# Splitting the reads of the sample states behind the first sequence's halves, sharing the page loads 12/11/9, and loading the first bias row a stage earlier, in a decoder step on one core

## The chip, the cores and the metric

The program runs on one NeuronCore of a Trainium2 chip. The metric is device time in microseconds (us), the median over several executions. Engines are called by their short names: PE (TensorE), ACT (ScalarE), DVE (VectorE), POOL (GpSimd) and SP (SyncE, which here only issues transfers). Everything is float32, and a float32 matmul stands in the trace as two matmul records with two weight loads.

## The reference, cut to what matters

One layer of a hybrid decoder is computed for a prompt of 1024 tokens and for 8 samples of 4 tokens. The change lies in the mLSTM of the samples and in the sparse attention:

```python
# mLSTM, one step for the samples (4 tokens each, 4 heads of 128)
num = sc[..., None] * einsum('bhvk,bhtk->bhtv', C, qc) + einsum('bhts,bhsv->bhtv', s, vc)
C = sc[..., -1, None, None] * C + einsum('bhs,bhsv,bhsk->bhvk', wl, vc, kc)

# sparse attention: each block of 32 cached tokens is compressed to one key and one value
blk = kb.reshape(B, nc, CMP_BLK, G, D) + pe[None, None, :, None, :]
flat = moveaxis(blk, 3, 2).reshape(B, nc, G, CMP_BLK * D)
kcmp = gelu(flat @ w1) @ w2      # and the same for the values
bias = rel_table[t5_bucket(dist)]  # added to every logit of the attention
```

For a sample the cached tokens lie in 32 pages of 128 tokens, scattered over a pool in DRAM. The page numbers are in `page_table`.

## The kernel before, in words

The whole step is one program of stages. Between two stages stands a barrier of all engines, ahead of which SP clears the semaphores of the stage one by one. Inside a stage each engine has its list of instructions written out by hand, and semaphores join the lists.

The change is in the joint stage `states_and_blocks` (tiles named `sab_...`), and in the stage behind it, `nsa_prompt` (tiles `np_...`). The joint stage does three things side by side:

- It compresses the cached blocks of 8 sequences. For sequence n the 32 pages (128 KB of each are needed) are loaded into `kv_in[n % 2]`, so there are two buffers. `load(eng, n, first, count, done)` issues one engine's share of the pages: for up to four pages at a time it reads the page numbers into registers (`value_load`, the TENSOR_LOAD rows), then issues one DMA per page. From n = 2 on the load waits until `layer1_ready` has reached 2(n-1), which is when PE has finished both halves of sequence n-2 and so released the buffer. PE then runs `first(n, 0)` and `first(n, 1)`, the first layer for keys and for values (64 matmul records each, helper `first_layer`), ACT applies the gelu, `second(n)` is the second layer, and DVE copies its result out (`blocks(n)`).
- It runs the mLSTM step of the samples: queries and keys, gates, `from_state` (the states C times the queries: 64 matmul records of 4 columns), `turn_inter`, `from_step`, `spread_scales`, and 8 `update(q)` of the states, which are put between the halves of the sequences.
- It does the prompt's own blocks (`own_first`, `own_second`, from the tile `sab_pairs`) and the vector of position biases: `bias_part` works in the tile `ring`, and SP writes the result to the DRAM scratch `bias_vec`.

The pages of a sequence are shared by the line

```python
SP_N, POOL_N, ACT_N = 14, 12, 6
```

The order of PE around the first sequences is written out:

```python
first(0, 0)
own_second()
from_state()
first(0, 1)
turn_inter()
first(1, 0)
```

ACT issues its pages behind the second gelu of the sequence whose buffer comes free, in the same list as its other work. `nsa_prompt` starts with SP loading two rows of `bias_vec` (one for each of two heads, 128 partitions x 1920 numbers each, read with a shift of one number from partition to partition) into `raw`. PE's first matmuls there wait for both rows, and nothing of the stage's attention starts before them.

Of the kernel before, what the change touches and what calls it, by code (L numbers as in the profile page):

```python
# [17 lines left out]
ACT = mybir.ActivationFunctionType  # L18
ALU = mybir.AluOpType
# [3 lines left out]
P = 128  # L23
# [904 lines left out]
RAWW = 1920  # L928
# [24 lines left out]
def states_and_blocks(nc, A, O, K, N, zn, hm, tokm, sm, pages, ring, tile_at, spare, c_at, psum):  # L953
# [6 lines left out]
    with stage(nc, "sab") as (ctx, sem):  # L960
# [7 lines left out]
        def dead(n, shape):  # L968
# [27 lines left out]
                 "updated", "norm_ready", "num_read", "square_ready", "root_ready", "gated_ready", "turned", "stored")  # L996
# [12 lines left out]
        SP_N, POOL_N, ACT_N = 14, 12, 6  # L1009
# [48 lines left out]
        def _(pe):  # L1058
# [150 lines left out]
        def _(act):  # L1209
# [10 lines left out]

            act.dma_start(mnorm[:, :, :], A["m_norm"].partition_broadcast(NS)).then_inc(S["small_loaded"], 16)
# [25 lines left out]
            gelu(0, 0)  # L1247
            act.wait_ge(S["inter_ready"], 1)
            nc.scalar.activation(inter[:, :, :], heads(psum[:, 7, 0:P]), ACT.Copy).then_inc(S["inter_copied"], 1)
            gelu(0, 1)  # L1250
            load(act, 2, SP_N, ACT_N, loaded)
            for n in range(1, NSEQ):
                gelu(n, 0)
                gelu(n, 1)
                if n == 1:
# [6 lines left out]
        def _(ve):  # L1262
# [62 lines left out]
            nc.vector.tensor_copy(N["vcmp"], psum[:, 2, P:2 * P]).then_inc(S["copied"], 1)  # L1325
            ve.wait_ge(S["inter_turned"], 1)
            ch.link(nc.vector.tensor_tensor(num[:, :, :], heads(psum[0:NS, 5, :]), per_head(sc[:, :], MD), ALU.mult))
            blocks(0)
# [15 lines left out]
            ve.wait_ge(S["inter_ready"], 1)  # L1344
            for n in range(1, 5):
                blocks(n)
                update(2 * n - 2)
                update(2 * n - 1)
# [2333 lines left out]
```

## Time and the profile before

| | us |
|---|---|
| median of 3 runs | 2687.54 |
| lowest, highest | 2683.41, 2691.82 |
| the profiled execution | 2690.47 |
| its span in the trace | 2688.8 |
| PE busy in the span | 2346.5 (87%) |
| joint stage, first DMA issue to last copy of DVE | 431.1 to 594.9 |
| start of the next stage, its first matmul | 598.7, 606.1 |

The profiled execution is one run, 2.93 us above the median. Times in the trace are counted from the start of the span. A row of the timeline merges neighbouring instructions of one line, so that its duration reaches from the start of the first to the end of the last. For a DMA on SP or ACT it is the time in which the engine issued them, not the time in which the data moved.

### The profile page before, as it was taken

To read this page: it belongs to the slowest core of one execution; us is meant where nothing else is said; L and a number is where in the kernel's file an instruction comes from. 1 tells how busy PE (TensorE), PEld (TensorE's weight loads), DVE (VectorE), ACT (ScalarE), POOL (GpSimd) and SP (SyncE) were. 2 spreads that over 40 slices of the span, in tenths; PEclk is the share of its full clock that TensorE was granted. 3 is DMA by queue.
4 is the path that set the end of the run, shared out by engine and by line. 5 is a ranking of instruction groups with operands and counts; after the bars stand their busy time and mean duration, and the time that the engine had idled before them with its cause. 6 is when DMAs were issued, how large, how long until landed. Compare 5 with 4: busy or idle time off the path is not lost. (4 is left out here: it accounts for less than half of the span.)

```text
span 2688.8 us, 41029 instructions
## 1 busy us (share of the span) xinstructions
PE 2346.5 (87%) x15785; PEld 2078.6 (77%) x15785; DVE 1086.2 (40%) x2456; ACT 691.7 (26%) x1391; POOL 393.8 (15%) x354
## 2 busy tenths in 40 slices
PE   8999676768999543999979988989999999999995
PEld 7799564665666321888879984879999999999995
DVE  2212453216777423211112610534755555553335
ACT  4210142004667211111113300344311111121123
POOL 0000021330000232111101110011122222212220
PEclk9999886788999766999989999999999999999997
DMA  3211205761300676111131013441211111111212
GB/s 130 106 40 40 14 1 172 229 232 60 122 22 1 206 245 220 37 35 47 39 112 32 32 48 109 195 154 53 76 55 48 48 48 42 45 38 48 106 42 73
DMA packets 118657, 228.71 MB, mean 85 GB/s; under 512 B 23666, under 2 KB 79635, under 8 KB 115299
## 3 DMA queue, kind: packets, MB, share of 16 engines
q1 hardware_dynamic: 85290, 171.55, 19.2%
q10 hardware_dynamic: 23970, 29.56, 3.2%
q0 software_dynamic: 9216, 25.18, 2.8%
q8 instruction: 114, 1.87, 0.3%
q14 instruction: 67, 0.55, 0.1%
HBM read 205.12 MB, written 25.31 MB: 86 GB/s over the span
## 5 line engine op out<-in xcount | busy, mean ns | idle before, releaser
L88 PE MATMUL psum<-x_half_high,ff_half 128*128 128x352 f32 x3240 | 790.9, 324 | 13.8 <-DVE h_again_low L69 8.9
L88 PEld LDWEIGHTS psum<-x_half_high,ff_half 128*128 128x128 f32 x3240 | 567.7, 189 | 15.1 <-DVE ff_half L69 9.1
L88 PE MATMUL psum<-h_again_low,ff_half 128*128 128x352 f32 x1176 | 379.2, 322 | 0.0
L69 POOL TENSOR_TENSOR ff_half<-ring,ff_half 128x1024 fp32r<-128x1024 f32 (+2 forms) x85 | 177.3, 2086 | 760.1 <-ACT ff_half L2987 760.1
L88 PEld LDWEIGHTS psum<-h_again_low,ff_half 128*128 128x128 f32 x1176 | 223.0, 190 | 0.0
L88 PE MATMUL psum<-x_half_high,mg_half 128*128 128x352 f32 x768 | 191.7, 330 | 22.2 <-ACTq L2117 22.2
L88 PE MATMUL psum<-merged_high,oq_half 128*128 128x352 f32 x768 | 190.8, 329 | 14.2 <-DVE oq_half L69 14.1
L2987 ACT ACTIVATE ff_half<-ring 128x1024 fp32r<-128x1024 f32 (+2 forms) x88 | 78.0, 888 | 433.1 <-PE psum L88 406.9
L88 PE MATMUL psum<-mid_low,ff_half 128*128 128x352 f32 x516 | 166.4, 323 | 0.0
L88 PEld LDWEIGHTS psum<-x_half_high,mg_half 128*128 128x128 f32 x768 | 135.1, 190 | 24.0 <-issue 22.4
L88 PEld LDWEIGHTS psum<-merged_high,oq_half 128*128 128x128 f32 x768 | 137.2, 193 | 15.1 <-DVE oq_half L69 14.7
L88 PE MATMUL psum<-h_high,in_half 128*128 128x352 f32 x528 | 126.1, 322 | 0.0
L88 PE MATMUL psum<-h_again_low,mg_half 128*128 128x352 f32 x384 | 124.1, 323 | 0.0
L2105 PE MATMUL psum<-low,mg_branch_w 128*128 128x352 f32 x384 | 116.2, 459 | 0.0
L88 PE MATMUL psum<-in_half,h_high 128*128 128x512 f32 (+3 forms) x360 | 102.1, 369 | 0.0
L938 PE MATMUL psum<-sab_kv,sab_w 128*64 128x128 f32 x1024 | 74.6, 316 | 31.0 <-DMA sab_kv<-in_pool 28.6
L2105 PEld LDWEIGHTS psum<-low,mg_branch_w 128*128 128x128 f32 x384 | 72.5, 190 | 37.2
L938 PEld LDWEIGHTS psum<-sab_kv,sab_w 128*64 128x64 f32 x1024 | 70.8, 164 | 35.7 <-DMA sab_kv<-in_pool 30.5
L3291 DVE TENSOR_TENSOR h_again<-h_again,psum 128x352 f32<-128x352 f32 x96 | 49.8, 520 | 119.4 <-PE psum L88 119.3
L88 PEld LDWEIGHTS psum<-mid_low,ff_half 128*128 128x128 f32 x516 | 97.6, 189 | 0.0
L1560 ACT ACTIVATE np_p<-np_p,np_nm 128x640 f32<-128x640 f32 (+7 forms) x128 | 92.7, 727 | 10.3 <-DVE np_nm L1632 10.0
L1511 PEld LDWEIGHTS psum<-consts,np_p 128*128 128x128 f32 x528 | 56.6, 142 | 49.9 <-DVE np_p L1662 21.1
(530 smaller groups left out, 3960.0 us busy)
## 6 DMA issues: line engine op xcount, KB each, us to landing
sab_kv<-in_pool SPq DMA_DIRECT2D x112, 128.0 KB, 3.5
sab_kv<-in_pool POOLq DMA_DIRECT2D x96, 128.0 KB, 3.8
ns_kv<-in_pool POOLq DMA_DIRECT2D x96, 128.0 KB, 4.6
ns_kv<-in_pool SPq DMA_DIRECT2D x96, 128.0 KB, 4.3
ring<-in_f_wu SPq DMA_DIRECT2D x22, 512.0 KB, 3.5
ring<-in_f_wg SPq DMA_DIRECT2D x22, 512.0 KB, 3.5
ns_kv<-in_pool ACTq DMA_DIRECT2D x64, 128.0 KB, 4.2
ring<-in_w_merge SPq DMA_DIRECT2D x16, 512.0 KB, 4.0
```

The source lines that it names most:

```text
L69: return engine.tensor_tensor(low, x, high.bitcast(F32), ALU.subtract)
L88: ins = nc.tensor.matmul(out, w[a], x[b], start=first and n == 0, stop=last and n == 2)
L938: last = nc.tensor.matmul(psum[g * HD:(g + 1) * HD, bank, 0:width], w1[:, kv, j, :], rows(g, j), start=(j == 0), stop=(j == CB // 2 - 1))
L1511: last = nc.tensor.transpose(psum[:, 4 + n % 2, c:c + P], src, K["ident"][:, :])
L1560: ins = nc.scalar.activation(x, x, ACT.Exp, bias=nm[:, b, g, i:i + 1], scale=-1.0, accum_out=sums[:, b, g:g + 1])
L2105: last = nc.tensor.matmul(acc[:, 3 + g, 0:GW], branch_w[:, r, k * P:(k + 1) * P], x[:, k, g * GW:(g + 1) * GW], start=(k == 0), stop=(k == 3))
L2987: nc.scalar.activation(half(u)[:, 0, 0:n], ring[:, u % 2, 0:n], ACT.Copy).then_inc(S["w_high"], 1)
L3291: ins = nc.vector.tensor_tensor(z[:, f, col(g)], z[:, f, col(g)], bank(v), ALU.add)
```

## The change

It has four parts. `from_state` takes a range of heads; heads 0 and 1 are read behind both halves of sequence 0, heads 2 and 3 behind `second(0)`. The items of the mLSTM step that follow it move on by one sequence (`update(0)` now stands in the pass of n = 3). The pages are shared 12 (SP), 11 (POOL), 9 (ACT). The two small transfers of `cmp_pe` into `sab_pairs` go from SP to the head of ACT's list. And the first of the eight bias rows is loaded in the joint stage, by SP behind its pages of sequence 2, into `ring`, which is free by then; in `nsa_prompt` the row for g = 0 always lives in `ring`.

```diff
-        SP_N, POOL_N, ACT_N = 14, 12, 6
+        SP_N, POOL_N, ACT_N = 12, 11, 9
...
             sp.dma_start(wqk[:, :, :, :], A["m_wqk"]).then_inc(S["wqk_loaded"], 16)
-            for g in range(2):
-                sp.dma_start(pairs[:, :, g, NPR:], A["cmp_pe"]).then_inc(S["pe_loaded"], 16)
...
             sp.dma_start(A["bias_vec"], onehot[0:NH, :]).then_inc(S["stored"], 16)
-            for n in range(2, NSEQ):
+            load(sp, 2, 0, SP_N, loaded)
+            sp.wait_ge(S["stored"], 16)
+            sp.dma_start(bias_row(ring, None)[0], bias_source(A, 0)).then_inc(S["raw_loaded"], 16)
+            for n in range(3, NSEQ):
                 load(sp, n, 0, SP_N, loaded)
+            sp.wait_ge(S["raw_loaded"], 16)
             sp.wait_ge(S["updated"], NSEQ)
...
-            def from_state():
+            def from_state(heads):
                 pe.wait_ge(S["C_loaded"], 16)
-                for h in range(MH):
+                for h in heads:
...
             first(0, 0)
             own_second()
-            from_state()
             first(0, 1)
-            turn_inter()
+            from_state((0, 1))
             first(1, 0)
             second(0)
+            from_state((2, 3))
+            first(1, 1)
+            turn_inter()
+            first(2, 0)
+            second(1)
             from_step()
-            first(1, 1)
+            first(2, 1)
             spread_scales()
-            for n in range(2, NSEQ):
+            for n in range(3, NSEQ):
                 first(n, 0)
                 second(n - 1)
-                if n < 6:
-                    update(2 * (n - 2))
-                if n == 6:
+                if n < 7:
+                    update(2 * (n - 3))
+                if n == 5:
                     turn_out()
                 first(n, 1)
-                if n < 6:
-                    update(2 * (n - 2) + 1)
+                if n < 7:
+                    update(2 * (n - 3) + 1)
...
+            for g in range(2):
+                act.dma_start(pairs[:, :, g, NPR:], A["cmp_pe"]).then_inc(S["pe_loaded"], 16)
             act.dma_start(mnorm[:, :, :], A["m_norm"].partition_broadcast(NS)).then_inc(S["small_loaded"], 16)
...
-            gelu(0, 0)
-            act.wait_ge(S["inter_ready"], 1)
-            nc.scalar.activation(inter[:, :, :], heads(psum[:, 7, 0:P]), ACT.Copy).then_inc(S["inter_copied"], 1)
-            gelu(0, 1)
-            load(act, 2, SP_N, ACT_N, loaded)
-            for n in range(1, NSEQ):
+            for n in range(NSEQ):
                 gelu(n, 0)
+                if n == 1:
+                    act.wait_ge(S["inter_ready"], 2)
+                    nc.scalar.activation(inter[:, :, :], heads(psum[:, 7, 0:P]), ACT.Copy).then_inc(S["inter_copied"], 1)
                 gelu(n, 1)
...
+def bias_row(ring, raw):
+
+    return ring[:, :, :].rearrange("p a k -> p (a k)")[:, 0:RAWW], raw
+
+
+def bias_source(A, h):
+    src = A["bias_vec"][h:h + 1, 0:RAWW]
+    return bass.AP(tensor=src.tensor, offset=src.offset, ap=[[1, P], [1, RAWW]])
...
-        raw = sb("raw", [P, 2, RAWW])
+        raw = bias_row(ring, sb("raw", [P, RAWW])[:, :])
...
-                    sp.dma_start(raw[:, g, :], src).then_inc(S["raw_loaded"], 16)
+                    if p or g:
+                        sp.dma_start(raw[g], bias_source(A, p + NPAIR * g)).then_inc(S["raw_loaded"], 16)
...
-                    pe.wait_ge(S["raw_loaded"], 32 * (p + 1))
+                    pe.wait_ge(S["raw_loaded"], 32 * p + 16)
```

On DVE the copies `blocks(0)` and `blocks(1)` and the updates move to match. The program's order of instructions shows it at three places. The first is PE, from the first half of sequence 0. Before (L938 is a half of a sequence, L1134 `from_state`, L1141 `turn_inter`, L1115 and L1116 `second`):

```order
L938 MATMUL psum<-sab_kv,sab_w_3303 64x128 x32
L1093 MATMUL psum<-sab_act_own,sab_w_3304 128x32
L1095 MATMUL psum<-sab_w_3304,sab_act_own 32x128 x4
L1134 MATMUL psum<-sab_qT,sab_C 128x4 x32
L938 MATMUL psum<-sab_kv,sab_w_3303 64x128 x32
L1141 MATMUL psum<-consts,sab_inter 32x128 x4
L938 MATMUL psum<-sab_kv,sab_w_3303 64x128 x32
L1115 MATMUL psum<-sab_act,sab_w_3304 128x128
```

The same place now (line numbers are those of the changed kernel, one higher or lower):

```order
L937 MATMUL psum<-sab_kv,sab_w_3303 64x128 x32
L1094 MATMUL psum<-sab_act_own,sab_w_3304 128x32
L1096 MATMUL psum<-sab_w_3304,sab_act_own 32x128 x4
L937 MATMUL psum<-sab_kv,sab_w_3303 64x128 x32
L1135 MATMUL psum<-sab_qT,sab_C 128x4 x16
L937 MATMUL psum<-sab_kv,sab_w_3303 64x128 x32
L1116 MATMUL psum<-sab_act,sab_w_3304 128x128
L1117 MATMUL psum<-sab_w_3304,sab_act 128x128
L1135 MATMUL psum<-sab_qT,sab_C 128x4 x16
L937 MATMUL psum<-sab_kv,sab_w_3303 64x128 x32
L1142 MATMUL psum<-consts,sab_inter 32x128 x4
```

The 32 matmuls of `from_state` have moved from ahead of the second half of sequence 0 to two places behind it, 16 each. The second place is the head of ACT's list in the joint stage. Before:

```order
L1208 UNCONDITIONAL_BRANCH
L1221 DMA sab_mnorm<-in_m_norm 32x512
L1222 DMA sab_n_3310<-in_s_n0t 32x512
L1223 DMA sab_n<-in_s_n 8x512
L1224 DMA sab_m<-in_s_m0t 32x4
L1018 TENSOR_LOAD pages
```

And now:

```order
L1213 UNCONDITIONAL_BRANCH
L1227 DMA sab_pairs<-in_cmp_pe 128x2x16 x2
L1228 DMA sab_mnorm<-in_m_norm 32x512
L1229 DMA sab_n_3310<-in_s_n0t 32x512
L1230 DMA sab_n<-in_s_n 8x512
L1231 DMA sab_m<-in_s_m0t 32x4
L1017 TENSOR_LOAD pages
```

Two transfers stand ahead of the four, and behind them ACT issues nine pages where it issued six, before its four copies into `sab_pairs` (`turn_pairs`). The third place is SP's list behind its last page of sequence 2, which is new:

```order
L1019 ISA
L1019 DMA sab_kv<-in_pool 128x256
L1042 DMA ring<-bias_vec 128x1920
L1017 TENSOR_LOAD pages
L1017 ISA x2
```

The bias row stands between the pages of sequence 2 and those of sequence 3.

## Rows read from the trace of the kernel before

**Rows 1.** The page: busy time and granted clock in 40 slices.

```profile
PE 2346.5 (87%) x15785; PEld 2078.6 (77%) x15785; DVE 1086.2 (40%) x2456; ACT 691.7 (26%) x1391; POOL 393.8 (15%) x354
PE   8999676768999543999979988989999999999995
```

**Rows 2.** Waits in the joint stage, 431 to 599; then SP's own waits.

```profile
PE psum L938 <- DMA sab_kv<-in_pool: 28.6, 6, 9.0
...
SPq L1018 <- PE psum L938: 16.1, 2, 13.0
...
SPq L123 <- DMA out_s_m<-sab_sl: 7.9, 1, 7.9
```

**Rows 3.** Timeline of PE, joint stage and after: start, duration, [idle before].

```profile
446.85 3.63 PE L938 MATMUL psum<-sab_pairs,sab_w 128*64 128x33 f32 x64
...
463.75 5.55 PE L938 MATMUL psum<-sab_kv,sab_w 128*64 128x128 f32 x64 [2.37 <-ACT sab_act_own L1244]
...
469.93 9.78 PE L1134 MATMUL psum<-sab_qT,sab_C 128*128 128x4 f32 x64
479.63 6.13 PE L938 MATMUL psum<-sab_kv,sab_w 128*64 128x128 f32 x64
...
491.52 3.71 PE L938 MATMUL psum<-sab_kv,sab_w 128*64 128x128 f32 x64
...
505.59 5.12 PE L938 MATMUL psum<-sab_kv,sab_w 128*64 128x128 f32 x64 [8.97 <-DMA sab_kv<-in_pool]
...
519.17 5.16 PE L938 MATMUL psum<-sab_kv,sab_w 128*64 128x128 f32 x64 [2.01 <-DMA sab_kv<-in_pool]
...
529.63 1.15 PE L1165 MATMUL psum<-tokm,sab_kwm 32*128 32x128 f32 x8
...
583.53 5.38 PE L938 MATMUL psum<-sab_kv,sab_w 128*64 128x128 f32 x64 [4.13 <-DMA sab_kv<-in_pool]
...
593.99 0.39 PE L1116 MATMUL psum<-sab_w,sab_act 128*128 128x128 f32 x2
606.08 6.08 PE L1485 MATMUL psum<-np_raw,consts 128*128 128x512 f32 x8 [11.71 <-DMA np_raw<-bias_vec]
```

**Rows 4.** Timeline of SP: issue of pages and transfers.

```profile
431.52 3.04 SPq L1033 DMA_DIRECT2D sab_pairs<-in_cmp_pe  x2
...
488.33 93.18 SPq L1020 DMA_DIRECT2D sab_kv<-in_pool  x84
581.56 0.43 SPq L1046 DMA_DIRECT2D out_s_C<-sab_C  x1
...
598.67 0.84 SPq L1434 DMA_DIRECT2D np_raw<-bias_vec  x2
```

**Rows 5.** Timelines of ACT and POOL: pages, copies.

```profile
437.07 4.35 ACTq L1020 DMA_DIRECT2D sab_kv<-in_pool  x6
441.47 2.65 ACT L1026 COPY sab_pairs<-zn 64x512 f32<-64x512 f32 x4 [16.27 <-issue]
...
488.10 4.07 ACTq L1020 DMA_DIRECT2D sab_kv<-in_pool  x6
...
493.46 2.29 POOL L1020 DMA_DIRECT2D sab_kv<-in_pool  x4 [2.24 <-issue]
```

**Rows 6.** DMA traffic in 490 to 503, then in 519 to 536.

```profile
DMA packets 3313, 4.01 MB, mean 308 GB/s; under 512 B 481, under 2 KB 2959, under 8 KB 3311
...
DMA packets 3917, 4.79 MB, mean 281 GB/s; under 512 B 569, under 2 KB 3480, under 8 KB 3916
```

**Rows 7.** Stretches: busy of PE, PEld, DVE (of sab_C's instructions), granted clock, DMA share, GB/s.

```profile
469.93:474.60 4.67, 4.67 (x41) 4.67 (x42) 0.00 (x0) 0.98 1.05 346
474.60:479.60 5.00, 5.00 (x24) 5.00 (x24) 0.00 (x0) 0.50 0.05 17
```

**Rows 8.** The bias rows' transfers: landing of the first, of the second (us).

```profile
np_raw<-bias_vec SPq DMA_DIRECT2D x1, 960.0 KB, 5.1
...
np_raw<-bias_vec SPq DMA_DIRECT2D x1, 960.0 KB, 7.0
```

More of the change, by code:

```diff
@@ L927 @@
 NCMP = TP // CB
-RAWW = 1920
 STRIPW, CSTRIPW, WSTRIPW = TP, NCMP + 4 * (NTILE - 1), WIN + P
@@ L995, in states_and_blocks @@
                  "inter_ready", "inter_copied", "inter_turned", "scale_ready", "scale_spread", "masked_ready", "update_ready",
-                 "updated", "norm_ready", "num_read", "square_ready", "root_ready", "gated_ready", "turned", "stored")
+                 "updated", "norm_ready", "num_read", "square_ready", "root_ready", "gated_ready", "turned", "stored", "raw_loaded")
         S = {n: sem(n) for n in names}
@@ L1325, in _ @@
             nc.vector.tensor_copy(N["vcmp"], psum[:, 2, P:2 * P]).then_inc(S["copied"], 1)
+            blocks(0)
             ve.wait_ge(S["inter_turned"], 1)
             ch.link(nc.vector.tensor_tensor(num[:, :, :], heads(psum[0:NS, 5, :]), per_head(sc[:, :], MD), ALU.mult))
-            blocks(0)
+            blocks(1)
             ve.wait_ge(S["intra_ready"], 1)
@@ L1343, in _, with nsa_prompt @@
             signal(nc.vector.tensor_tensor(n8[:, :, :], n8[:, :, :], heads(psum[0:NSEQ, 4, :]), ALU.add), "norm_ready")
-            ve.wait_ge(S["inter_ready"], 1)
-            for n in range(1, 5):
+            ve.wait_ge(S["inter_ready"], 2)
+            for n in range(2, 6):
                 blocks(n)
-                update(2 * n - 2)
-                update(2 * n - 1)
-            ve.wait_ge(S["root_ready"], 1)
-            ch.link(nc.vector.reciprocal(r1[:, :], r1[:, :]))
-            ch.link(nc.vector.tensor_tensor(num[:, :, :], num[:, :, :], per_head(r1[:, :], MD), ALU.mult))
-            ch.link(nc.vector.tensor_tensor(num[:, :, :], num[:, :, :], mnorm[:, :, :], ALU.mult))
-            signal(nc.vector.tensor_tensor(num[:, :, :], num[:, :, :], heads(tokm[0:NS, last, C_OG:C_OG + 512]), ALU.mult), "gated_ready")
-            blocks(5)
-            ve.wait_ge(S["turned"], 1)
-            nc.vector.tensor_copy(hm[:, :, TP:T], heads(psum[:, 5, 0:P]))
+                update(2 * n - 4)
+                if n == 2:
+                    ve.wait_ge(S["root_ready"], 1)
+                    ch.link(nc.vector.reciprocal(r1[:, :], r1[:, :]))
+                    ch.link(nc.vector.tensor_tensor(num[:, :, :], num[:, :, :], per_head(r1[:, :], MD), ALU.mult))
+                    ch.link(nc.vector.tensor_tensor(num[:, :, :], num[:, :, :], mnorm[:, :, :], ALU.mult))
+                    signal(nc.vector.tensor_tensor(num[:, :, :], num[:, :, :], heads(tokm[0:NS, last, C_OG:C_OG + 512]), ALU.mult), "gated_ready")
+                update(2 * n - 3)
+                if n == 4:
+                    ve.wait_ge(S["turned"], 1)
+                    nc.vector.tensor_copy(hm[:, :, TP:T], heads(psum[:, 5, 0:P]))
             blocks(6)
             blocks(7)
-def nsa_prompt(nc, A, O, K, N, zn, tokn, gates, on, psum):
+RAWW = 1920
+def bias_row(ring, raw):
[3 more added lines that the diff above has]
+    return bass.AP(tensor=src.tensor, offset=src.offset, ap=[[1, P], [1, RAWW]])
+def nsa_prompt(nc, A, O, K, N, zn, tokn, gates, on, ring, psum):
     BIAS = -1
@@ L1484, in scores @@
                                 c = slice(i * 512, i * 512 + w) if i < 2 else slice(CB - 1, CB + CB * (CSTRIPW - 1), CB)
-                                last = nc.tensor.matmul(out, K["flip"][:, :], raw[:, g, c], start=True, stop=True)
+                                last = nc.tensor.matmul(out, K["flip"][:, :], raw[g][:, c], start=True, stop=True)
                             elif br == CMP:
@@ L3479, in build @@
             assert place["blocks_kept"] == place["tokm"]
-            nsa_prompt(nc, A, O, K, N, zn, tokn, branch_gates, zm, psum)
+            nsa_prompt(nc, A, O, K, N, zn, tokn, branch_gates, zm, ring, psum)
             nsa_sample(nc, A, K, N, zn, tokn, branch_gates, pages, zm, psum)
```

5 lines of the change are left out of this document (1 added, 4 removed).

## The prediction

> **What bounds the kernel now.** I read the page first. PE is busy for 87% of the span, so most of the time is matmul work that this change doesn't touch; but its busy digits fall to 5, 4 and 3 in slices seven to ten, and its clock digits there to 6 and 7 [rows 1]. The joint stage lies in these slices, so I read only that stage. The list of waits says what PE lacks there: 28.6 us in six waits for pages of the cache, the longest 9.0 [rows 2]. The timeline of PE shows where they stand: ahead of the first half of each sequence from the third on, with 8.97 us at 505.59 and still 4.13 us at 583.53 [rows 3]. From 519.17 to 583.53 four sequences pass, 16.1 us each.
>
> Next, who is late with the pages. SP issues 84 of them in 93.18 us with hardly a pause, 1.11 us a page [rows 4], and in the whole stage it waits for PE only twice, 16.1 us together, 13.0 of them ahead of sequence 2 [rows 2]. So a load of 14 pages takes SP 15.5 us. POOL needs 2.29 + 2.25 = 4.5 us for four pages, 13.6 us for its twelve. ACT starts 2.3 us after the release at 485.76 (the end of the row at 479.63) and issues six pages in 4.07 us, 6.4 us in all, 1.07 a page, and is done long before the others [rows 3, 5]. SP is the last of the three by 2 us against POOL and by 9 against ACT. What remains, from the end of SP's issue to PE's start, I call the tail: 485.76 + 15.5 = 501.3, PE starts at 505.59, so 4.3 us.
>
> The other gate is the buffer. The pages of sequence 2 can only be issued once PE has finished sequence 0, at 485.76, and between its two halves stand the 9.78 us of reading the states [rows 3]. Meanwhile SP stands idle. The stretches show something more: in the first part of this read the granted clock was 0.98 of full speed, in the second 0.50, the lower of the two levels, 1.2 GHz [rows 7]. The first part did 41 matmul records in 4.67 us, the second 24 in 5.00, and the half sequence behind it took 6.13 us where a warm one takes 3.71 [rows 3, 7].
>
> **The change part by part.** Times on the old clock of the trace.
>
> *Opening.* ACT gets two small transfers at its head and three pages more. SP's own pair took 3.04 us, in which one issue had stalled [rows 4]; without a stall two cost about 0.6. Three pages cost 3 x 1.07 = 3.2. ACT's copies into the pairs ended at 441.47 + 2.65 = 444.1 [rows 5]; they will end at 447.9 to 450.3. PE needs them at 446.85 for the prompt's own blocks [rows 3], so a cover of 2.7 us is used up and PE comes 1.1 to 3.5 us later. I take +2.5, nearer the stall, since it has been seen with these very transfers. SP's list gets shorter, but nothing waits for its first pages: PE is late for other reasons. The release for sequence 1 moves with PE; its pages are still in time, because PE now comes to them later in its list.
>
> *Order.* Sequence 0: the first half starts at 463.75 + 2.5 = 466.3, ends 5.5 later, the prompt's second layer takes 0.7, the second half, now warm, 3.7: done at 476.2 against 485.76. Behind it stand half the state read (16 matmuls, 32 records: 3.6 us at full clock, 6.7 at half; I take 3.7, since warm halves now stand between them), a half of sequence 1 (3.7), the second layer (0.6), the other read (3.7) and the other half (3.7): sequence 1 is released at 491.6, and before it was at 491.52 + 3.71 = 495.2. Everything from the state read to the updates moves on by one sequence. DVE and ACT wait for it there, but both idle most of the stage, so I cost it at nothing.
>
> *Shares.* SP's load: 12 x 1.11 = 13.3 us, POOL's 12.5, ACT's 9 x 1.07 = 9.6. The time from release to PE's start was 19.8 for sequence 2. By the issue it becomes 13.3 + 4.3 = 17.6. By the data: 32 pages of 128 KB are 4.19 MB; in 490 to 503, when all three queues fed it, the traffic was 308 GB/s [rows 6], which makes 13.6 us; with 2.6 from the release to SP's first issue (488.33 [rows 4]) and 2.0, about half of the tail, for a page to be under way, 18.2. The later of the two counts: 18.2. Its bounds are 17.0 (the traffic rises as the shares get even) and 19.5 (281 GB/s, as in 519 to 536 [rows 6]).
>
> One rule of the Trainium skill speaks against this part: in "DMA: Bandwidth & Descriptors", section "Issuing engines are not separate DMA queues", it is said that issuing on several engines saves only the sequencers' time, usually small beside the transfer. Here 1.11 us on SP stands against 0.43 us of traffic for a page at 308 GB/s, so the trace doesn't agree with "small"; the rest of the rule is my first rival. By the same page's limit of about 358 GB/s for a core's HBM, an estimate for a sequence would be 11.7 us of traffic.
>
> *The sum in the stage.* PE needs 529.63 - 519.17 = 10.5 us from the start of a sequence to its release [rows 3]. With two buffers, sequences 3, 5 and 7 form one chain: 491.6 + 18.2 = 509.8; + 10.5 + 18.2 = 538.5; + 28.7 = 567.2. SP issues the pages of 4 and 6 between, 13.3 us each, and is free again at 518.2 and 546.9, before the releases at 520.3 and 549.0, so it isn't in the way. Against 583.53 [rows 3] this is -16.3, and the rest of the stage (10.8 us to 594.4) is unchanged. A period is 14.3 us in place of 16.1.
>
> *What is late next.* SP writes out the states at 581.56 and then waits 7.9 us for these writes, to about 9.2 behind the first issue [rows 2, 4]. Now the last update is done behind sequence 6, near 565, and the write ends near 574, before PE at 578. It costs nothing, but only 4 us cover it.
>
> *Bias row.* 960 KB in the joint stage, between two loads of SP, near 490; it falls where the pages of sequence 3 wait for their release anyway: 0, at most its own 3 us of traffic once. In the next stage PE starts at 606.08, when the second of two rows lands, 7.0 us after its issue; the first landed after 5.1 [rows 8]. One row alone, issued at 598.7, lands at 603.8: -2.3.
>
> *Sum:* -16.3 - 2.3 = -18.6. From the profiled execution, 2690.47, that gives 2671.9. It was 2.93 above the median of the runs, so 2669.0.
>
> **The rivals.** *First, the DMA engines are the bound.* Then even shares only make the pages queue longer: the whole tail of 4.3 stands behind 13.6 us of traffic, 20.5 a load, and the chain ends at 574.1, -9.4; with the bias row -11.7, so 2675.8. At 281 GB/s it is 21.8, -5.5 and -2.3, so 2679.7. For it: 308 GB/s with three queues falls short of the 346 of a stretch in [rows 7], so something else than issue limits it, too. Against: ACT was done after 6.4 us of each load, and from then on two queues fed the engines. Chance 0.18.
>
> *Second, what is won is lost again within the kernel.* The opening costs its full 3.5, the clock falls in both state reads (6.7 each, +6.0 on the release of sequence 1), and the first gates gain nothing; only a period shorter by 1.8 remains for four sequences, -7.2, and -2.3, with some 3 of it lost in the opening: about -6.5, so 2681. For it: the clock did fall within this read [rows 7]. Chance 0.08.
>
> *Third, slower.* ACT becomes the last. Its pages stand in one list with the gelus, so that every page waits behind them, and every later gelu behind the pages. It takes the load over from 13.9 us on (18.2 less the tail), 1.54 a page against 1.07 now. To make the kernel slower by 8 us the chain has to end 10.4 later than before, 27.1 us a load, 2.5 us a page on ACT; then the time is 2696. Against: six pages took it 4.07 and 4.35 us in the two loads shown, while SP and POOL were issuing, too [rows 5]. Only the stalled pair came near such a price. Chance 0.04.
>
> **How the numbers follow.** My own case has the other 0.70: load times of 17.0 to 19.5 and an opening of 1.1 to 3.5 give -23.6 to -13.7, 2664 to 2674; the median of a few runs adds 4 us either way. The range for 8 in 10 reaches into the first rival: 2661 to 2680. This kernel's measurement tells about 0.3%, 8 us, from no change; 2679.5 is that border. Most of the first rival is faster still, the second is about the border: faster 0.85, within 0.3% 0.11, slower 0.04.
>
> **What would show it.** Right: PE's first half of sequence 2 near 494, of 3 near 510, of 7 near 567, with waits for pages remaining ahead of sequences 3 to 7, but shorter; SP with waits for PE between its loads; the own blocks of the prompt starting near 449; the state read in two pieces of under 4 us at full clock; the first bias matmul 5.1 us after the start of its stage. Wrong: traffic above 300 GB/s throughout with the time from release to start at 20 us or more (first rival); two state reads at clock 0.5 (second); ACT still issuing when SP has finished (third).

## The result, and the profile after

| | before | after |
|---|---|---|
| median, us | 2687.54 | 2672.87 |
| lowest, highest of the runs | 2683.41, 2691.82 | 2669.97, 2675.89 |
| the profiled execution, its span | 2690.47, 2688.8 | 2675.89, 2674.2 |

The ratio of the changed kernel to the one before is 0.9945, with a 95% interval of 0.9931 to 0.9959: faster by 14.8 us (11.0 to 18.5). The forecast was 2669.0 with a range of 2661 to 2680. In the main the mechanism came as forecast, but the joint stage gave less than its term, and a part of the total came from a place that the forecast didn't name. The rest of this document finds out where.

Here is the page of the changed kernel (busy time; granted clock in 40 slices), and below it the clock of the kernel before, since the second line of [rows 1] is PE's busy share and not its clock:

```profile
PE 2338.6 (87%) x15785; PEld 2074.8 (78%) x15785; DVE 1086.7 (41%) x2456; ACT 691.2 (26%) x1391; POOL 389.9 (15%) x346
PEclk9999885879999776999989999999999999999997
```

```profile
PEclk9999886788999766999989999999999999999997
```

PE does the same 15785 matmul records in 7.9 us less. The work is the same and the mean granted clock of the execution was 0.929 against 0.927, which fits less time at the lower clock. The waits of the joint stage (engine, what it waited for: us in all, times, longest):

```profile
PE psum L937 <- DMA sab_kv<-in_pool: 23.7, 3, 8.5
...
SPq L1017 <- PE psum L937: 26.0, 5, 10.3
```

SP now waits for PE five times, 26.0 us in all, where it waited twice, 16.1. Six waits of PE for pages have become three, but these are nearly as long: 23.7 us against 28.6 [rows 2]. The timeline of PE says how:

```profile
447.83 3.63 PE L937 MATMUL psum<-sab_pairs,sab_w 128*64 128x33 f32 x64 [1.50 <-ACT sab_pairs L1025]
...
471.61 3.71 PE L937 MATMUL psum<-sab_kv,sab_w 128*64 128x128 f32 x64
475.25 3.74 PE L1135 MATMUL psum<-sab_qT,sab_C 128*128 128x4 f32 x32
478.92 5.38 PE L937 MATMUL psum<-sab_kv,sab_w 128*64 128x128 f32 x64
484.78 4.75 PE L1135 MATMUL psum<-sab_qT,sab_C 128*128 128x4 f32 x32
489.46 5.85 PE L937 MATMUL psum<-sab_kv,sab_w 128*64 128x128 f32 x64
495.79 3.72 PE L937 MATMUL psum<-sab_kv,sab_w 128*64 128x128 f32 x64
...
514.09 5.49 PE L937 MATMUL psum<-sab_kv,sab_w 128*64 128x128 f32 x64 [7.92 <-DMA sab_kv<-in_pool]
...
526.08 3.71 PE L937 MATMUL psum<-sab_kv,sab_w 128*64 128x128 f32 x64
...
544.74 5.53 PE L937 MATMUL psum<-sab_kv,sab_w 128*64 128x128 f32 x64 [8.49 <-DMA sab_kv<-in_pool]
...
574.27 6.11 PE L937 MATMUL psum<-sab_kv,sab_w 128*64 128x128 f32 x64 [7.24 <-DMA sab_kv<-in_pool]
580.95 3.71 PE L937 MATMUL psum<-sab_kv,sab_w 128*64 128x128 f32 x64
...
595.33 2.08 PE L1503 MATMUL psum<-ring,consts 128*128 128x512 f32 x2 [9.49 <-DMA np_raw<-bias_vec]
```

Sequence 0 is released at 475.3 (471.61 + 3.71), but sequence 1 only at 495.3, where it was before. Its two halves took 5.38 and 5.85 us and the second state read 4.75, where each was costed near 3.7. From then on the sequences go in pairs: 3, 5 and 7 wait 7.2 to 8.5 us, and 4 and 6 follow at once. The stretches around the reads and over the pairs (us, busy of PE, PEld, DVE, ACT, POOL, then granted clock, DMA share, GB/s) are these:

```profile
475.20:478.90 3.70, 3.70 (x36) 3.65 (x32) 0.00 (x0) 0.37 (x1) 0.43 (x1) 1.00 0.28 83
481.00:484.80 3.80, 3.80 (x41) 3.63 (x38) 0.00 (x0) 0.00 (x0) 1.65 (x4) 0.65 0.99 306
484.80:487.20 2.40, 2.40 (x24) 2.40 (x23) 0.49 (x2) 0.37 (x1) 0.71 (x2) 0.97 0.99 289
487.20:489.50 2.30, 2.30 (x13) 2.28 (x13) 0.00 (x0) 0.00 (x0) 1.40 (x3) 0.50 1.01 345
506.00:519.00 13.00, 5.08 (x59) 4.91 (x60) 1.70 (x4) 3.00 (x4) 5.90 (x11) 0.61 1.08 351
519.00:537.00 18.00, 17.20 (x244) 15.65 (x240) 9.02 (x19) 1.36 (x4) 6.57 (x13) 1.00 0.76 241
537.00:553.00 16.00, 8.26 (x96) 7.93 (x98) 2.50 (x6) 0.37 (x1) 6.91 (x13) 0.68 1.04 339
553.00:569.00 16.00, 14.03 (x210) 12.96 (x204) 6.07 (x12) 0.99 (x3) 5.90 (x11) 1.00 0.66 213
```

The first read ran at full clock. In the half sequence behind it the mean was 0.65, it was back at 0.97 when the second read began, and by the end of that read it was 0.50, the lower of the two levels, 1.2 GHz. Over the pairs, PE is busy at full clock while the DMA engines have gaps (241 and 213 GB/s), and in turn with this PE waits while they run full (351 and 339). The mean over a whole pair is only a little above that of before: 282 GB/s in 513 to 544, against 267 in 519 to 583 of the kernel before. How long a page is under way changed, too. These are all pages issued in 505 to 570, first of the kernel before (number of pages, size, median us from issue to landing):

```profile
sab_kv<-in_pool SPq DMA_DIRECT2D x56, 128.0 KB, 3.3
sab_kv<-in_pool POOLq DMA_DIRECT2D x48, 128.0 KB, 3.4
sab_kv<-in_pool ACTq DMA_DIRECT2D x24, 128.0 KB, 3.2
```

and of the changed one:

```profile
sab_kv<-in_pool SPq DMA_DIRECT2D x52, 128.0 KB, 4.3
sab_kv<-in_pool POOLq DMA_DIRECT2D x47, 128.0 KB, 4.7
sab_kv<-in_pool ACTq DMA_DIRECT2D x37, 128.0 KB, 4.5
```

Pages are issued sooner and are under way 1.0 to 1.3 us longer. The issue on SP and ACT (start, us of issuing, times):

```profile
430.94 1.35 ACTq L1227 DMA_DIRECT2D sab_pairs<-in_cmp_pe  x2
...
437.60 7.39 ACTq L1019 DMA_DIRECT2D sab_kv<-in_pool  x9
445.04 2.64 ACT L1025 COPY sab_pairs<-zn 64x512 f32<-64x512 f32 x4 [20.00 <-issue]
```

```profile
477.89 11.58 SPq L1019 DMA_DIRECT2D sab_kv<-in_pool  x12
...
497.71 72.13 SPq L1019 DMA_DIRECT2D sab_kv<-in_pool  x60
569.94 0.37 SPq L1047 DMA_DIRECT2D out_s_C<-sab_C  x1
...
590.06 0.35 SPq L1452 DMA_DIRECT2D np_raw<-bias_vec  x1
```

### The profile page after: what moved, and what is told of

Read it like the earlier page. It is cut to its first block and busy times, and to the rows that moved or that the text cites. A ratio compares the mean times of both kernels' runs of the same rounds, so it can differ in the third digit from the quotient of the medians.

```text
span 2674.2 us, 41030 instructions
## 1 busy us (share of the span) xinstructions
PE 2338.6 (87%) x15785; PEld 2074.8 (78%) x15785; DVE 1086.7 (41%) x2456; ACT 691.2 (26%) x1391; POOL 389.9 (15%) x346
## 3 DMA queue, kind: packets, MB, share of 16 engines
q1 hardware_dynamic: 82442, 169.42, 19.3%
## 5 line engine op out<-in xcount | busy, mean ns | idle before, releaser
L88 PE MATMUL psum<-merged_high,oq_half 128*128 128x352 f32 x768 | 190.4, 329 | 14.9 <-DVE oq_half L69 14.8
L88 PEld LDWEIGHTS psum<-x_half_high,mg_half 128*128 128x128 f32 x768 | 135.0, 190 | 23.9 <-issue 22.3
L937 PE MATMUL psum<-sab_kv,sab_w 128*64 128x128 f32 x1024 | 71.8, 308 | 26.1 <-DMA sab_kv<-in_pool 23.7
L1529 PE MATMUL psum<-consts,np_p 128*128 128x128 f32 x528 | 79.2, 284 | 16.9 <-ACT np_pt L1592 10.2
```

The lines of the kernel that those rows point to most:

```text
L88: ins = nc.tensor.matmul(out, w[a], x[b], start=first and n == 0, stop=last and n == 2)
L937: last = nc.tensor.matmul(psum[g * HD:(g + 1) * HD, bank, 0:width], w1[:, kv, j, :], rows(g, j), start=(j == 0), stop=(j == CB // 2 - 1))
L1529: last = nc.tensor.transpose(psum[:, 4 + n % 2, c:c + P], src, K["ident"][:, :])
```

## The experiments

Two measures are used. The ratio is that of times, with its interval. "Stage" is the length of the joint stage in one profiled execution, from PE's first own block to the end of its last half sequence. The profiled execution is one run and lies up to 6 us from its kernel's median. Much of this lies outside the stage: the span behind the first bias matmul, work that the experiments leave as it was but for where later bias rows are loaded to, took 2073.0 to 2083.5 us (last column). But PE's halves around the state reads differ from trace to trace by some 3 us, too, as is shown further down, so one stage length settles nothing below a few us.

| kernel | ratio to before, 95% | stage, us | profiled less median | behind the first bias matmul, us |
|---|---|---|---|---|
| before | 1 | 146.3 | +2.9 | 2082.7 |
| after | 0.9945 [0.9931, 0.9959] | 136.8 | +3.0 | 2078.9 |
| e1, shares alone | 0.9983 [0.9970, 0.9996] | 142.7 | +6.2 | 2082.6 |
| e2, order alone | 0.9968 [0.9955, 0.9982] | 137.4 | +4.8 | 2083.4 |
| e3, bias row alone | 0.9990 [0.9980, 1.0000] | 143.7 | -1.7 | 2080.7 |
| e4, before, constant page numbers | 0.9998 [0.9983, 1.0013] | 145.1 | +1.3 | 2079.3 |
| e5, e4 with loads in turn | 0.9992 [0.9981, 1.0002] | 143.5 | +2.7 | 2083.5 |
| e6, after, state read later | 0.9938 [0.9920, 0.9956] | 134.1 | +0.5 | 2078.8 |
| e7, after, early numbers | 0.9928 [0.9910, 0.9946] | 128.1 | -5.6 | 2075.3 |
| e8, e7 with loads in turn | 0.9955 [0.9937, 0.9974] | 140.3 | 0.0 | 2076.0 |
| e9, e6 and e7 together | 0.9915 [0.9898, 0.9933] | 125.1 | +1.0 | 2081.4 |
| e10, after, constant page numbers | 0.9938 [0.9920, 0.9955] | 135.6 | +1.5 | 2077.0 |
| e11, before, early numbers | 0.9984 [0.9972, 0.9996] | 142.5 | -4.3 | 2073.0 |
| e12, e7 with shares 14/12/6 | 0.9928 [0.9911, 0.9946] | 133.1 | +4.4 | 2083.3 |

### The change taken apart: e1, e2, e3

**e1**, the kernel before with one line changed:

```diff
-        SP_N, POOL_N, ACT_N = 14, 12, 6
+        SP_N, POOL_N, ACT_N = 12, 11, 9
```

> The kernel before with one line changed: pages shared 12/11/9 in place of 14/12/6. My theory (issue on SinceE's list sets the load, 2.2 us less for two pages fewer): the time from a release to the first half falls from 19.8 to about 18, a period from 16.1 to about 15, the chain of sequences 3, 5 and 7 ends 5 to 7 us earlier; the opening costs 0.5 to 1. Total -4 to -7 us, ratio near 0.998. Rival (the DMA engines are the bound, the shares only move the queue): the time from release to start stays at 19.5 or more and the total is within 2 us of before.

It gained 4.6 us (ratio; 1.1 to 8.1), as the theory had it. But the theory's reason didn't come: from the release of sequences 0, 2 and 4 to PE's start of 2, 4 and 6 it took 20.0, 19.8 and 19.3 us, the rival's sign, and not 18. The time was won otherwise: sequences 3, 5 and 7 follow sequences 2, 4 and 6 at once or nearly so, so they come in pairs (its timeline of PE):

```profile
511.71 6.32 PE L938 MATMUL psum<-sab_kv,sab_w 128*64 128x128 f32 x64 [9.09 <-DMA sab_kv<-in_pool]
...
524.41 3.71 PE L938 MATMUL psum<-sab_kv,sab_w 128*64 128x128 f32 x64
...
543.23 5.93 PE L938 MATMUL psum<-sab_kv,sab_w 128*64 128x128 f32 x64 [8.65 <-DMA sab_kv<-in_pool]
```

**e2**, the changed kernel with three of its four parts undone, so that only the order is left:

```diff
-        SP_N, POOL_N, ACT_N = 12, 11, 9
+        SP_N, POOL_N, ACT_N = 14, 12, 6
...
-            sp.dma_start(bias_row(ring, None)[0], bias_source(A, 0)).then_inc(S["raw_loaded"], 16)
```

(with `cmp_pe` back on SP and both rows loaded in `nsa_prompt`).

> Only the new order of PE, ACT and DVE (state reads in two pieces behind the halves), with shares 14/12/6, the small transfers on SP and both bias rows in the later stage. My theory: sequence 0 is released 9 to 10 us earlier than before, but sequence 1 at about 494 as before, since the clock falls to 0.5 in the reads; so only part is kept: the stage ends 4 to 8 us earlier. Rival (the release of sequence 0 is all that counts): the whole 9.5 us arrive at the end of the stage.

It gained 8.6 us (4.8 to 12.1), the largest part, a little more than the theory's 4 to 8. As expected, sequence 1 was released at 494.6 only; the gain came although that was as late as before, because SP began on the pages of sequence 3 at 497.0 and not at 503.5: from the release of sequence 1 to the start of 3 it took 19.4 us, and 23.9 before. Between the theory and the rival's 9.5 us this run can't decide. The move of the two small transfers wasn't run by itself.

**e3**, the kernel before with the first bias row loaded in the joint stage:

```diff
+            sp.wait_ge(S["stored"], 16)
+            sp.dma_start(bias_row(ring, None)[0], bias_source(A, 0)).then_inc(S["raw_loaded"], 16)
```

> The kernel before with the first bias row loaded in the joint stage, nothing else. My theory: the first bias matmul starts 5.2 us after its stage in place of 7.4, -2.2 us, and the joint stage is as long as before; total -2 to -3 us. Rival (a transfer of 960 KB in the joint stage delays the pages behind it): the joint stage becomes 1 to 3 us longer, and nothing remains.

It gained 2.7 us, with an interval that ends at no gain (1.0000), and the joint stage didn't pay for it: 143.7 us against 146.3. Its sequences paired as well, with waits of 9.86, 0.74, 8.47, 0.65, 9.21 and 1.48 us ahead of sequences 2 to 7, though its shares were the old ones and its sequence 1 was released at 495.2 as before. The three parts add to 4.6 + 8.6 + 2.7 = 15.9 against 14.8 for the whole.

### Is it the issue or the traffic: e4, e5, e10

**e4**, the kernel before with constant page numbers in place of the table's. It compresses other pages than the reference:

```diff
-                page = [eng.value_load(pages[0:1, n * NPAGE + e:n * NPAGE + e + 1], min_val=0, max_val=N["n_pool"] - 1) for e in some]
+                page = [n * NPAGE + e for e in some]
```

> The kernel before with page numbers that are constants of the program (page 32n+e, so other pages than the table names): the same transfers without the reads of page numbers, which halves what an engine issues a page in (1.11 to about 0.55 us on SP). Theory that issue is the bound: a load takes SP 8 us in place of 15.5, and the stage falls to what PE and the traffic allow: periods of 13 to 14 us, stage 12 to 18 us shorter. Rival (the traffic is the bound already): a period stays above 15.5 and the stage falls by less than 5 us.

The theory fell and the rival held: the time didn't change. SP was relieved, as its own waits say:

```profile
SPq L1020 <- PE psum L938: 57.7, 7, 21.0
```

It waits 57.7 us for releases where it waited 16.1 [rows 2]. But the pages issued in 505 to 570 then took 6.2 to 7.0 us to land, twice as long as before, and PE's waits became fewer and longer:

```profile
509.40 6.01 PE L938 MATMUL psum<-sab_kv,sab_w 128*64 128x128 f32 x64 [7.67 <-DMA sab_kv<-in_pool]
...
543.91 5.82 PE L938 MATMUL psum<-sab_kv,sab_w 128*64 128x128 f32 x64 [11.96 <-DMA sab_kv<-in_pool]
```

The stretches of e4 show the shape, full traffic and then a gap:

```profile
530.00:545.00 15.00, 3.04 (x34) 2.68 (x32) 1.76 (x3) 0.37 (x1) 6.36 (x12) 0.65 1.08 348
545.00:560.00 15.00, 15.00 (x208) 14.12 (x205) 4.01 (x8) 0.85 (x3) 4.58 (x9) 0.89 0.35 111
```

**e5**, e4 with each load also waiting until the load before it has landed:

```diff
+                eng.wait_ge(loaded[(n - 1) % 2], 16 * (SP_N + ACT_N) * ((n - 1) // 2 + 1))
+                eng.wait_ge(loaded_soft[(n - 1) % 2], 16 * POOL_N * ((n - 1) // 2 + 1))
```

> The kernel before with constant page numbers (other pages than the table names, as in the run before this one), and one wait more: every engine's load of sequence n waits until all pages of sequence n-1 have landed. My theory now (two loads in flight share the DMA engines, so the earlier one lands late and PE gets two sequences at once): in turn, each load has the engines to itself and takes 12 to 13 us of traffic and 2.5 of start, a period of 14.5 to 15.5 in place of 17.2, the joint stage 8 to 14 us shorter than without the wait. Rival (the traffic is the bound, whatever its order): a wait more can only leave the DMA engines idle for longer, a period above 17 and the stage as long or longer.

The sequences came evenly, 15.6 us apart (505.18 to 583.04 in five periods of its timeline). But that is no gain: in e4 a pair takes 34.5 us, and yet from the start of sequence 2 at 509.40 to that of sequence 7 at about 588.6 it is 15.8 us a sequence, since no wait stands between the two of the last pair. So the stage was only 1.6 us shorter and the time the same: the theory's 8 to 14 us didn't come, and neither did the rival's period above 17. From 505 to 583 the mean traffic of e5 was 284 GB/s (e4 had 267 in 509.4 to 578.4), where the full stretch of e4 has 348: one load after the other leaves gaps as well, between the last page of one and the first of the next.

**e10**, the edit of e4 on the changed kernel.

> The changed kernel with constant page numbers (32n + e in place of the table's), so that no engine reads a number; it compresses other pages than the reference. Shared traffic with a start for each pair of loads: the start shrinks by the 2.2 to 2.6 us of the number reads and the issue by half, so it does at least what the early numbers did, a joint stage of 126 to 130 us and a pair of sequences in 26 to 28 us. Rival, from the same edit on the kernel before, which gave nothing: pages issued faster only come in denser bursts with longer gaps, the pair stays at 30 us or more and the stage at 135 us or more.

The rival held for the stage, 135.6 us, and the time was that of the changed kernel (0.9938 against 0.9945); the two pairs took 31.6 and 27.6 us, between the theory's 26 to 28 and the rival's 30 or more. Its pages, issued in 505 to 570:

```profile
sab_kv<-in_pool SPq DMA_DIRECT2D x43, 128.0 KB, 8.8
sab_kv<-in_pool POOLq DMA_DIRECT2D x39, 128.0 KB, 6.6
sab_kv<-in_pool ACTq DMA_DIRECT2D x31, 128.0 KB, 9.6
```

Issued as fast as this, they are under way 1.4 to 2.1 times as long as in the changed kernel. The time that the issue saved came back as time under way. That the pages of e4 and e10 are other ones could have a part in this, too, and these runs can't tell the two apart.

### The start of a load: e7, e11, e12, e8

**e7**, the changed kernel, in which the first four page numbers of a load are read ahead of its wait for the release (nothing of the computation changes):

```diff
-            if n == 1:
-                eng.wait_ge(S["own1_ready"], 2)
-            if n >= 2:
-                eng.wait_ge(S["layer1_ready"], 2 * (n - 1))
             for at in range(first, first + count, 4):
...
+                if at == first and n == 1:
+                    eng.wait_ge(S["own1_ready"], 2)
+                if at == first and n >= 2:
+                    eng.wait_ge(S["layer1_ready"], 2 * (n - 1))
```

> The changed kernel with the first four page numbers of each load read ahead of its wait for the buffer in place of behind it. Theory that the start of a load is on the path once for each pair of sequences: 2.2 us less for each of the loads of 3, 5 and 7, the stage 5 to 7 us shorter. Rival (traffic bound): the loads only overlap more, 0 to 2 us.

The ratio went to 0.9928, some 4.6 us below the changed kernel, though the two intervals overlap. The stage of 128.1, 8.7 us shorter, flatters it: up to 3.3 us of this is the clock around the state reads, which the edit doesn't touch (from the release of sequence 0 to that of 1 it took 16.7 us, and 20.0 in the changed kernel's trace). The loads of sequences 5 and 7 did get shorter, 16.3 and 16.7 us from release to start against 19.8 and 18.4; that of sequence 3 didn't, 19.8 against 18.8.

**e11**, the same edit on the kernel before.

> The kernel before, with its shares 14/12/6 and its order, and only the first page numbers read ahead of the wait. If SP's issue sets the pace there (it waits for PE twice in the stage), early numbers save at most the reads ahead of sequence 2, 2.3 us, and the joint stage is 0 to 3 us shorter than 146.3. Rival: the start of every load counts whatever the shares are, and the stage is 6 to 8 us shorter, as it was in the changed kernel.

It gained 4.3 us (1.1 to 7.5), and the stage was 3.9 shorter: between the two theories, a little above mine. The interval doesn't exclude mine, so that SP's issue isn't the only thing that set the pace in the kernel before is likely and not shown.

**e12**, e7 with the old shares.

> The changed kernel with early numbers, but with the shares 14/12/6. If SP's issue is the bound at these shares, a sequence takes 15.5 us again in place of 13.6, and the joint stage is 8 to 12 us longer than the 128.1 of the early numbers with 12/11/9. Rival: with the numbers read early the shared engines are the bound at any shares, and the stage is at most 3 us longer.

The theory's 8 to 12 us didn't come. Whether the rival holds is open, since the two measures disagree: the stage is 5.0 longer than in e7 and a sequence takes 14.8 us against 13.6, with the clock around the state reads the same in both traces (16.7 us from release to release). But the ratios are equal, 0.9928, each known to some 5 us. So a gain of the even shares beside early numbers isn't shown, and up to some 5 us isn't excluded.

**e8**, e7 with each load behind the landing of the one before, by the two waits of e5.

> As the run with early page numbers, and in addition each load waits until the one before has landed. Theory of shared traffic: the pairs dissolve, every sequence is waited for by itself, a period of 14 to 14.8 us against 15.3 in the changed kernel, the stage 3 to 7 us shorter than the changed kernel's. Rival: each load starts later than it could, a period of 16 or more, the stage longer by 4 us or more.

It came out slower than e7, 0.9955, with intervals that overlap a little, and its sequences came 16.3 us apart (516.51 to 581.73 in four periods), where those of e7 came 13.6 apart (513.85 to 568.13). So my expectation fell and the rival held nearly (a stage 3.5 us longer than the changed kernel's, where it asked for 4): in these two kernels the overlap of two loads was worth more than their order. Between e4 and e5 there was no such difference, 15.8 against 15.6.

### The place of the state read: e6, e9

**e6**, the changed kernel with the whole read behind both halves of sequence 1, so that no narrow matmul stands ahead of either release:

```diff
-            from_state((0, 1))
             first(1, 0)
             second(0)
-            from_state((2, 3))
             first(1, 1)
-            turn_inter()
+            from_state((0, 1))
+            from_state((2, 3))
             first(2, 0)
+            turn_inter()
             second(1)
```

(ACT's copy of what was read moves behind its pages of sequence 3.)

> The changed kernel with the whole state read moved behind both halves of sequence 1, where PE waits for pages anyway. Theory that the release of sequence 1 (495.2, delayed by two reads and a slow clock) is what the change left on the path: it comes near 484, and the stage ends 4 to 8 us earlier than in the changed kernel. Theory of shared traffic: sequences 2 and 3 are released 8 to 9 us apart, both loads fly at once, sequence 2 starts later than 494 and only 0 to 3 us remain.

Sequence 1 was released at 488.4 in place of 495.3. But the read, 10.14 us, now stood ahead of sequence 2, and of the 6.9 us about 2 reached the time (0.9938 against 0.9945, within the intervals). The stage was 2.8 us shorter, and sequences 2 and 3, 4 and 5, 6 and 7 came as pairs: the expectation's theory of shared traffic (0 to 3 us) held, and that of the release (4 to 8 us) didn't.

**e9**, e6 and e7 together.

> The changed kernel with both edits that helped by themselves: the first page numbers of each load are read ahead of its wait, and the whole read of the states stands behind both halves of sequence 1. If they act at different places (the one at the start of every load, the other at the release of sequence 1), they add: a joint stage of 125 to 127 us where the early numbers alone gave 128.1, and 2667 to 2669. Rival: the release of sequence 1 doesn't matter once the loads overlap better, because the data of sequence 3 queue behind those of sequence 2 in any case: the stage stays at 128 and the time at 2670.

As expected: a stage of 125.1 us, a median of 2668.03, a ratio of 0.9915. It is the fastest kernel of this study; its interval reaches 0.9933, that of the changed kernel begins at 0.9931. Its timeline of PE from the state read on:

```profile
486.51 10.36 PE L1135 MATMUL psum<-sab_qT,sab_C 128*128 128x4 f32 x64
...
524.89 5.16 PE L937 MATMUL psum<-sab_kv,sab_w 128*64 128x128 f32 x64 [5.43 <-DMA sab_kv<-in_pool]
...
538.08 5.38 PE L937 MATMUL psum<-sab_kv,sab_w 128*64 128x128 f32 x64 [1.58 <-DMA sab_kv<-in_pool]
...
565.68 5.23 PE L937 MATMUL psum<-sab_kv,sab_w 128*64 128x128 f32 x64 [2.05 <-DMA sab_kv<-in_pool]
```

From sequence 4 on the sequences no longer pair: they come 13.6 us apart, with waits of 1.6 to 2.1.

## Why the prediction was right, and where it was off

**The reading of the page.** The opening paragraph puts busy digits of 5, 4 and 3 into slices seven to ten. They stand in slices 14 to 16, which are another stage; slices seven to ten, where the joint stage lies, have 6, 7, 6 and 8, and clock digits of 6, 7, 8 and 8. The argument doesn't suffer, since it goes by the waits and the timeline of the stage.

**Order.** The release of sequence 0 was forecast for 476.2 and came at 475.3. The release of sequence 1 was forecast for 491.6 and came at 495.3. The step that failed is "I take 3.7, since warm halves now stand between them", together with the 3.7 taken for each half behind a read. The first read did keep full clock, but the half behind it, the second read and the half behind that took 5.38, 4.75 and 5.85 us, 16.0 together against 3 x 3.7 = 11.1; part was saved by the earlier start. This is the cause that I had given to the second rival (at its full price of 6.0 us there, about 3.7 here). e6 supports it: with the reads out of the way the two halves of sequence 1 took 3.71 each. How much it costs differs from trace to trace, and the changed kernel's is one of the two dearest. Six kernels have this order of PE, and from the release of sequence 0 to that of sequence 1 they took 20.0 us (the changed kernel, e8), 18.4 (e2) and 16.7 (e7, e10, e12), where the forecast had 15.4. In the last four the second read took 3.63 us. In e10 the half behind it was warm, too:

```profile
484.85 3.63 PE L1135 MATMUL psum<-sab_qT,sab_C 128*128 128x4 f32 x32
488.41 3.71 PE L937 MATMUL psum<-sab_kv,sab_w 128*64 128x128 f32 x64
```

In each of the six at least one of the two halves took 5.3 us or more.

**Shares and load time.** Forecast 18.2 us from release to start, bounds 17.0 and 19.5; measured 18.8, 19.8 and 18.4 for sequences 3, 5 and 7 (from the PE rows above: 514.09 - 495.31, and so on). The size was off by 0.8 in the mean. A piece of the first rival fits this: pages issued sooner were under way longer, 4.3 to 4.7 us against 3.2 to 3.4. The whole rival, 20.5 a load, didn't come. What I had missed is the pairing: two loads run side by side, so the traffic is full in bursts (339 to 351 GB/s) with gaps between. Even shares alone bring it about (e1), but so did the bias row alone in e3, with old shares and the old release, so what sets it off is open. Nor is it shown to cost anything by itself: e1 and e3 pair, and both were, if anything, faster than the kernel before. The Trainium skill ("DMA: Bandwidth & Descriptors", section "Issuing engines are not separate DMA queues") says that issuing from several engines saves only sequencer time, since all share the same 16 DMA engines. With faster issue than the changed kernel's (e4, e10) this case agrees; its "usually small" doesn't fit here: a page took 1.11 us on SP [rows 4] against 0.37 us of traffic at 351 GB/s, and early numbers alone gained 4.3 us in e11.

**The sum.** In the chain of sequences 3, 5 and 7 the last start was 574.27 against 567.2 forecast, 7.1 late: 3.7 from the release of sequence 1, 2.4 from three loads, 1.0 from PE's own time (10.9 and 11.1 us a sequence where 10.5 was taken). So the stage's term of -16.3 measured -9.3 at that row, and -8.5 at the last half sequence, because this one ran partly cold. That -9.3 is near the first rival's -9.4 is chance: by this sum about half of the shortfall, 3.7 of 7.1, is the clock around the state reads. The sum says where this trace lost time, not what would come back: in e6 sequence 1 was released 6.9 us earlier and only about 2 us reached the end.

**The opening.** PE's own blocks began 1.0 us later (447.83), where 2.5 was forecast, just under the lower bound of 1.1. Counted from the stage's first DMA issue (430.93 against 431.10) it is 1.2 later. The two small transfers took 1.35 us on ACT, without the stall of [rows 4]; the 0.6 that I had given for two without a stall was too low, since on SP they took 1.27 in e2 as well. ACT's nine pages took 7.39, 3.0 more than six, as forecast (3.2). At 0.8 to 0.9 us a page in the later loads (7.4 to 8.1 us for nine) ACT stayed far from the third rival's 2.5.

**Bias row.** The next stage's first matmul stands 5.27 us behind SP's issue of its row (595.33 - 590.06). Before it was 7.41 (606.08 - 598.67), so -2.1 against -2.3 forecast. e3 has the same 5.3 and gained 2.7 by itself. Loading it in the joint stage cost nothing that can be seen.

**States' write.** Issued at 569.94, it costs nothing, as forecast: from the end of PE's last half sequence (584.66) to SP's first issue in the next stage stand 5.4 us, and 5.5 stood there before (593.20 to 598.67).

**What made up for it was luck.** The first bias matmul came 10.8 us earlier, but the span is 14.6 shorter. The other 3.8 us lie behind this matmul, in work that the change leaves as it was but for where its later bias rows are loaded to. The largest piece there is a stretch in `nsa_prompt` at half clock, first of the kernel before, then of the changed one:

```profile
617.80:631.50 13.70, 10.97 (x42) 5.20 (x43) 8.30 (x38) 7.31 (x25) 0.26 (x1) 0.50 0.06 24
```

```profile
606.70:613.50 6.80, 3.95 (x15) 2.05 (x15) 4.90 (x23) 3.78 (x14) 0.38 (x1) 0.51 0.15 63
```

It shrank from 13.7 to 6.8 us. All 14 traces have this stretch, some 9 to 13 us behind the first bias matmul: in seven it lasts 13 to 14 us (before, e1, e2, e4, e5, e9, e12), in six about 7 (after, e6, e7, e8, e10, e11), in e3 about 10. The bias row doesn't decide it. Here is e11, which has both rows in the later stage as before, then e9, which has the row early:

```profile
615.10:621.40 6.30, 3.64 (x14) 2.02 (x14) 4.54 (x22) 3.44 (x13) 0.18 (x1) 0.50 0.07 29
```

```profile
596.50:609.50 13.00, 9.80 (x38) 4.91 (x40) 8.69 (x37) 6.71 (x24) 0.72 (x1) 0.50 0.11 45
```

With the long stretch the span behind the first bias matmul was 2082.3 us in the mean of the traces, with the short one 2076.5. So the 3.8 us are within what this stretch gives or takes from trace to trace, and nothing here shows that the change brought them. The forecast had no term for it, and by it the traced total came out closer (-14.6 against -18.6) than the stage did. Whether a kernel gets the same stretch in each of its executions can't be told from one trace each.

**What stays open.** Shares and early numbers each gained about 4.5 us on the kernel before (e1, e11). With order and bias row they aren't additive. Order and bias row alone come to 8.6 + 2.7 = 11.3 (a sum, not a run); with the shares the gain is 14.8, with early numbers and old shares 19.3 (e12), with both 19.3 (e7). A reading that fits is that both shorten the same thing, the time until a load's last page is issued, and that below this the shared traffic decides; the traces of e7 and e12 (13.6 against 14.8 us a sequence) speak against a full overlap of the two. Why issue with constant numbers gains nothing on the kernel before where early numbers do isn't settled. One reading fits e10: when all three queues are issued far ahead, the pages of the next load compete with the last pages of the present one. The Trainium skill (same page, section "Queues, rings and completion order") says that each DMA engine goes round robin between queues, which would let ACT's short list reach the next load while SP's is still busy with this one. No run here looked at the order of landing, and the constant numbers also name other pages, so this is argued and not shown.

## What to carry to other kernels

When transfers for two buffers are issued faster, look at how long each is under way as well as at how long its issue takes: here 3.3 us a page before, 4.5 after and 6.6 to 9.6 in e10 went with less and less gain from issue. Put address reads ahead of the wait that gates a load, so that the first transfer leaves at the release: that gained about as much as dividing the pages anew (4.3 and 4.6 us), and beside it the times show no further gain from the division. Keep narrow matmuls out of the path to a buffer's release, as their cost also falls on the wide ones behind them. And before you explain the last few us of a total, look at a stretch that the change doesn't touch in several traces: here one alone gave or took about 6 us.

## What the runs showed of the hardware

- In the changed kernel the granted clock fell behind the first of two state reads (0.65 in the half sequence behind it) and again within the second (0.50 at its end), although each had only 32 records of 4 columns. With the same order of PE the second read kept its 3.63 us in four of six traces. The clock fell in the one long read of e9 as well (10.36 us), where the stretch from 491.5 to 496.8 has 0.50.
- The same work of `nsa_prompt` has a stretch at clock 0.50 that lasts 13 to 14 us in seven traces and about 7 in six, and the span behind it differs by some 6 us with it.
- The traffic of pages had a ceiling here: 339 to 351 GB/s in the full stretches of the changed kernel and of e4, at a DMA share of 1.04 to 1.08. A sequence of 4.19 MB needs 12.0 us at that; the best period reached was 13.6 us (e7, e9). A stretch of e9 with the bias row in flight beside pages reached 378 GB/s.
- Overlapping loads beat loads in turn in e7 against e8 (13.6 us a sequence against 16.3), although the data moved are the same. In e4 against e5 they didn't (15.8 against 15.6).
